# Hybrid RWKV-7 / short-convolution block with top-4-of-32 experts: GpSimd gathers expert rows two rounds ahead, in the middle of the round, and scatters behind that

## What is computed

```python
logits = xf @ w_router + b_router                 # 32 experts
top_v, top_i = lax.top_k(logits, 4); gates = softmax(top_v)
# assignments are grouped by expert, in blocks of up to 128 rows
xb = xf[toks]                                     # rows of one expert
gt = minimum(xb @ w_e_gate[e] + b_e_gate[e], 7)
up = clip(xb @ w_e_up[e] + b_e_up[e], -7, 7)
act = (up + 1) * (gt * sigmoid(1.702 * gt))
y = (act @ w_e_down[e] + b_e_down[e]) * wts[:, None]
out = zeros.at[row_tok].add(y)
```

## Time and profile before

| | before |
|---|---|
| median of 3 runs | 3091.75 us |
| the profiled execution | 3067.25 us |
| its span | 3065.6 us |
| PE busy | 2798.6 us (91%) |
| DVE busy | 1789.7 us (58%) |
| ACT busy | 1361.6 us (44%) |
| POOL busy | 514.2 us (17%) |
| mean granted TensorE clock | 0.955 |

### The profile page before, as it was taken

One profiled execution on the slowest core, in us unless ns is written; L12 is line 12 of the kernel. 1 busy time (PEld: TensorE's weight loads), 2 busy tenths in 40 slices (PEclk: granted clock), 3 DMA queues, 4 the chain that ended last, 5 costly groups with the idle time before them and its releaser, 6 DMA issues.

```text
span 3065.6 us, 55893 instructions
## 1 busy us (share of the span) xinstructions
PE 2798.6 (91%) x21371; PEld 2340.7 (76%) x21371; DVE 1789.7 (58%) x1990; ACT 1361.6 (44%) x1501; POOL 514.2 (17%) x511
## 2 busy tenths in 40 slices
PE   7999999999998999796899999999899999999993
PEld 6797878878898999443688878888777777777772
DVE  3456546464422121143576776767788888888885
ACT  2423232232211111032565666665666666666664
POOL 1010101010000000123132323232222212222220
PEclk9999999999999999897899999999999999999996
DMA  3000000000012110522677868777988888988887
GB/s 105 21 2 15 8 8 15 2 22 1 28 41 56 41 41 21 156 67 70 230 280 257 282 248 283 257 281 264 352 324 323 323 327 330 353 331 329 327 331 245
DMA packets 143212, 536.25 MB, mean 175 GB/s; under 512 B 17633, under 2 KB 71239, under 8 KB 90125
## 3 DMA queue, kind: packets, MB, share of 16 engines
q1 hardware_dynamic: 122925, 492.74, 43.4%
q0 software_dynamic: 20192, 42.08, 5.6%
HBM read 500.35 MB, written 34.42 MB: 174 GB/s over the span
## 4 chain that ended last, share of the span: by engine, by line
PE 71%; DMA 14%; issue 7%; DVE 3%; POOL 2%; ACT 2%; POOLq 1%; SPq 0%; ACTq 0%; DVEq 0%
PE bank L839 30%; PE bank L1958 8%; PE bank L1959 7%; PE bank L1960 7%; DMA x_rows<-hn_d,next_t 6%; DMA next_t<-slot_d 5%; PE bank L1967 5%; PE bank L1871 4%; PE bank L1936 2%; PE bank L835 2%; POOL mid_t L1496 2%; PE bank L915 2%; DMA wo_t<-in_w_o 1%; PE bank L1946 1%; PE bank L2028 1%
## 5 line engine op out<-in xcount | busy, mean ns | idle before, releaser
L1789 DVE TENSOR_TENSOR w_lo<-raw_first,w_hi 128x2048 fp32r<-128x2048 f32 x275 | 618.3, 2283 | 73.7 <-ACT w_hi L1584 73.6
L1584 ACT ACTIVATE w_hi<-raw_first 128x2048 fp32r<-128x2048 f32 x276 | 529.5, 1919 | 228.1 <-DMA raw_first<-in_w_e_up 63.4
L1958 PE MATMUL bank<-w_hi,x_hi 128*128 128x512 f32 x1088 | 434.0, 399 | 2.4 <-ACT yo_rows L1632 2.4
L1959 PE MATMUL bank<-w_lo,x_hi 128*128 128x512 f32 x1088 | 425.1, 391 | 0.0
L1960 PE MATMUL bank<-w_hi,x_lo 128*128 128x512 f32 x1088 | 424.8, 390 | 0.0
L1789 DVE TENSOR_TENSOR w_lo<-raw_rest,w_hi 128x2048 fp32r<-128x2048 f32 x136 | 307.8, 2282 | 0.2
L1584 ACT ACTIVATE w_hi<-raw_rest 128x2048 fp32r<-128x2048 f32 x136 | 260.8, 1917 | 100.8 <-PE bank L1994 43.4
L839 PE MATMUL bank<-xm_hi,ring_hi 128*128 128x260 f32 x896 | 261.9, 292 | 16.2 <-DVE dz L791 8.2
L839 PE MATMUL bank<-xm_lo,ring_hi 128*128 128x260 f32 x896 | 255.0, 285 | 0.0
L839 PE MATMUL bank<-xm_hi,ring_lo 128*128 128x260 f32 x896 | 255.0, 285 | 0.0
L1958 PEld LDWEIGHTS bank<-w_hi,x_hi 128*128 128x128 f32 x1088 | 204.8, 188 | 51.2 <-issue 10.4
(11 more groups left out here) (364 smaller groups left out, 4706.3 us busy)
## 6 DMA issues: line engine op xcount, KB each, us to landing
raw_first<-in_w_e_up SPq DMA_DIRECT2D x138, 1024.0 KB, 5.9
raw_first<-in_w_e_gate SPq DMA_DIRECT2D x70, 1024.0 KB, 6.4
raw_rest<-in_w_e_gate SPq DMA_DIRECT2D x70, 1024.0 KB, 5.6
raw_first<-in_w_e_down SPq DMA_DIRECT2D x68, 1024.0 KB, 6.3
raw_rest<-in_w_e_down SPq DMA_DIRECT2D x68, 1024.0 KB, 8.7
ring<-in_w_in SPq DMA_DIRECT2D x40, 512.0 KB, 3.9
hn_d<-hn SPq DMA_DIRECT2D x10, 416.0 KB
h_d<-h_all SPq DMA_DIRECT2D x10, 416.0 KB
```

The source lines that it names most:

```text
L1584: nc.scalar.activation(w_hi[:, j % NRING, :, :], raw_piece(j), ACT.Copy).then_inc(hi_done, 1)
L1789: nc.vector.tensor_tensor(w_lo[:, j % NRING, :, :], raw_piece(j), w_hi[:, j % NRING, :, :].bitcast(f32), ALU.subtract).then_inc(lo_done, 1)
L1958: nc.tensor.matmul(ps[:, :], hi, w_hi[:, slot, k, :], start=start and k == 0, stop=False)
L1959: nc.tensor.matmul(ps[:, :], hi, w_lo[:, slot, k, :], start=False, stop=False)
```

## The change

GpSimd now asks in the middle of round r for the rows of round r + 2, right after TensorE has transposed those of round r + 1. A second gather stands ahead of the loop. The order in a round becomes: wait for the scatter of round r - 1, copy to `slot_t`; wait for the rows of round r + 1, copy to `mid_t`; wait for the transposes of round r + 1's rows; `gather(r + 2)`; wait for piece 9, biases of round r + 1; scatter round r. No buffer and no transfer is added but one further gather, past the last round.

```diff
         gather(0, True)
         get_biases(0)
+        pool.wait_ge(rows_in[0], 16)
+        pool.wait_ge(rows_in[1], 16)
+        nc.gpsimd.tensor_copy(mid_t, next_t).then_inc(mid_kept, 1)
+        nc.gpsimd.tensor_copy(mid_ov, next_ov).then_inc(mid_kept, 1)
+        pool.wait_ge(mid_kept, 2)
+        pool.wait_ge(xT_ps[3], 1)
+        gather(1, True)
         pool.wait_ge(h_out, 16 * NT)
         for first, last, wide in ((0, n_wide, True), (n_wide, rounds, False)):
             with pool.Fori(first, last) as r:
-
-                pool.wait_ge(rows_in[0], r * 16 + 16)
...
-                pool.wait_ge(xT_ps[3 if wide else 1], r + 1)
-                gather(r + 1, wide)
 
                 pool.wait_ge(y_out[0], r * 16 + 16)
                 pool.wait_ge(y_out[1], r * 32 + 32 if wide else n_wide * 32 + 32)
...
+                pool.wait_ge(rows_in[0], r * 16 + 32)
+                pool.wait_ge(rows_in[1], r * 16 + 32 if wide else n_wide * 16 + 32)
                 pool.sem_inc(pool_passed, 1)
+                nc.gpsimd.tensor_copy(mid_t, next_t).then_inc(mid_kept, 1)
+                if wide:
+                    nc.gpsimd.tensor_copy(mid_ov, next_ov).then_inc(mid_kept, 1)
+                    pool.wait_ge(mid_kept, r * 2 + 4)
+                else:
+                    pool.wait_ge(mid_kept, r + n_wide + 3)
+                pool.sem_inc(pool_passed, 1)
+
+                pool.wait_ge(xT_ps[3 if wide else 1], r + 2)
+                gather(r + 2, wide)
 
                 if wide:
                     pool.wait_ge(ov_used, r * NPIECE + 10)
...
-        pool.wait_ge(rows_in[0], rounds * 16 + 16)
+        pool.wait_ge(rows_in[0], rounds * 16 + 32)
```

## The result

The changed kernel takes 3035.72 us (median of 4 runs, 3033.07 to 3046.09) against 3087.54 for the kernel before (4 runs, 3081.65 to 3095.08). The ratio is 0.9837, 95% interval 0.9802 to 0.9872: faster by 52 us or 1.6%, where 16 us were forecast. The profiled execution took 3033.96 us, 33 less than the profiled one of before. From the scatter on, the code stands five lines further down: L1535 is the L1530 of before, L1941 is L1936 and L1999 is L1994.

What follows compares the result with a forecast made beforehand. PE was taken to bound the wide rounds; in single rounds a scatter-list-gather-PE loop made PE wait, with PE, DMA engines and VectorE near each other. Terms -90 + 74 = -16 us from 3091.75 gave 3076, range 3003 to 3132.

Steps and rivals of the forecast that it cites:

- its loop from scatter to scatter: Single rounds: scatter, list, gather, PE, scatter form a loop that sets the round at 41.1 us.
- The list, behind it in the same queue, lands about 1 us later: Single rounds: the scatter lands at 2500.8, the list about 1 us later, so the gather is issued only at 2502.62.
- Term 1: Single rounds: the wait for gathered rows goes, round 41.1 to 36.8 us, -90 us over 21 rounds (bounds -115 to -44).
- Term 2: Wide rounds: bias load behind the gather comes late, stall 4.0 us plus 1.7 for the clock, +74 us over 13 rounds.
- The rest is moved at no cost: Scatter, copies, SyncE's loads and GpSimd's instruction count: the remaining moves in the round cost 0.
- Biases in time in the wide rounds: Rival, wide rounds: the bias load causes no stall, giving 3002 us; chance 0.20.
- Biases late in the single rounds: Rival, single rounds: biases come 1.5 us late, plus 1.7 for the clock, +67 us, giving 3143; chance 0.17.
- the cover of 2 us: Single rounds: biases land 15.1 us behind the transposes' end, PE wants them at 17; cost 0.
- The DMA engines as the bound: Rival, single rounds: DMA engines hold the round at 39.0 us, -44 + 74 = +30, giving 3122; chance 0.13.

Runs made afterwards that it cites:

- experiment 8: Kernel before, GpSimd's order untouched; in single rounds PE transposes the next rows ahead of piece 10 instead of 8: 2977.78 us against 3083.68, ratio 0.9664.
- experiment 4: Kernel before, with the list for the next round read by ScalarE on its own queue: 3093.27 us, ratio 1.0086.
- experiment 5: Kernel before, with the scatter of the single rounds cut to 16 of its 128 rows: 3052.58 us beside 3080.68.
- experiment 7: Kernel after, loading only half of each weight piece in the single rounds: 3037.55 us.
- Experiment 1: Kernel after, with the biases loaded ahead of the wait for the transposes and the gather, in both loops: 2975.29 us against 3064.4, ratio 0.9695.
- experiment 2: Kernel after, with the bias load issued between the list reads and the two indirect gathers: 2974.31 us, ratio 0.9699.
- experiment 6: Kernel before, loading only half of each weight piece in the single rounds: 2995.36 us beside 3080.68.
- experiment 3: Order of the kernel before in the wide rounds, changed order in the single ones, one gather between the loops: 2961.74 us against 3064.4, ratio 0.9666.
- Experiment 9: Kernel after, with the bias load moved behind the scatter as the last thing of the round: 3335.57 us beside 3080.68.

## Why the prediction was right, and where it was off

**The forecast.** 3076 with a range of 3003 to 3132; measured 3036, inside, and on the side that had the largest chance. The sum was -16 and the medians say -52, so it is right in its two main terms and off in size. Of the 36 us between, 18 are term 1, -5 are term 2, 4 are what counting rounds leaves of the 33 between the profiled executions, and 19 are the spread between executions of before, which the forecast had no term for. By its own two terms as measured it would have come to -29; that the median lies near the low end of the forecast's own range of 3035 to 3115 is in part luck.

**What bounds the kernel.** The forecast's reading, a wait for the rows in every single round and no wait in the wide ones, held, and so did its loop from scatter to scatter: the chain under experiment 8 goes round it. But what is in the loop is the scatter's issue, since GpSimd takes the copy and the list only behind it, and not its landing. "The list, behind it in the same queue, lands about 1 us later" is true of the times and reads as a cause. As a cause it fell: in a queue of its own the list took 8.2 us (experiment 4), and with the scatter landing 4.4 us earlier it came 1.2 us earlier (experiment 5). The list takes 7.0 us because of the weight loads and the scatter in flight together, and 4.6 with half of the one or without the other (the table under experiment 7). The forecast wanted 2 to 4 us for it after the change and it was 4.6. The number wasn't harmed, because the term came from the stall and the clock.

**Term 1** was forecast at -90 and is -108. The term of the sum that was mis-sized is the round that is left, 36.8 us, from a floor of 36.3 us of DMA work and an allowance for two full resources. The round takes 35.94 us, less than that floor, with the same bytes in it (331 x 41.1 against 381 x 35.9). The allowance was for nothing: half the traffic leaves the round at 35.93 (experiment 7). And the share was no measure of work: with 54% of the bytes (205 against 381 GB/s) the share was still 0.65 against 0.99, 66%. The other half of the step, the stall, was read from one round. Its 3.8 us is 3.5 on average (73.6 / 21), and 41.1 - 3.5 - 1.7 = 35.9 us is what was measured, 0.3 above the forecast's 35.6 for TensorE.

**Term 2** was forecast at +74, with +79 in the traces, and is right in mechanism as well; that it is so close is partly luck, as two sizes off by 0.5 and 1.5 us and one round too many offset each other. Issue of the bias load: 6.6 us behind the list (1588.22 - 1581.66), forecast 1892.0 for a list at about 1885, so 7; from the end of the transposes, 7.9 us (1588.22 - 1580.29) against 8.4. Landing: PE goes on 7.3 us behind the issue, near the upper of the two values named (7.7), where 5.8 was taken. Stall 4.65 us (4.0), and 58.4 - 51.8 - 4.65 = 1.9 us of clock and others (1.7). Experiment 1 takes only the bias load out of its place, and 5.2 us a round come back. By the Trainium skill (DMA: Bandwidth & Descriptors, Anatomy of one DMA) the landing would have been 2.1 us, an estimate from its fit, and the term +4. In the wide rounds of these kernels no bias load comes near that (4.9 us at the least, experiment 2); with half of the weight loads, in the single rounds of experiment 6, it was 2.9. The Trainium skill (DMA: Bandwidth & Descriptors, Queues, rings and completion order) leaves room for a later transfer to complete before an earlier one. No run here shows a bias load doing so: it was slower by 2.1 us behind the gathers than ahead of them, by 2.5 behind the full scatter than behind a small one, and landed 0.2 us behind the full one.

**"The rest is moved at no cost"** stands half open. The gather's new place in the wide rounds seemed to cost 1.4 us: 53.2 us in experiment 1 against 51.9 in experiment 3, whose medians lie 13.5 us apart in one set of runs. But 53.0 to 53.7 us, with the same wait for `a_lo`, were also seen where the wide loop was untouched. Which of them it is, the runs don't settle. For the single rounds the statement held: they take 35.94 us with PE busy all the time.

**The rivals.** Biases in time in the wide rounds: refuted, 12 waits. Biases late in the single rounds: no such wait in the first profile of the kernel after, and two short ones of 1.6 and 0.2 us in the second, at the start of the single rounds; how much of the cover of 2 us was left isn't shown, as no view gives the landing there. Experiment 9 is the price when it doesn't hold. The DMA engines as the bound: refuted by half the loads in the kernel after (experiment 7).

**Left open.** The rounds give -29, the profiled executions -33 and the medians -52 and -50. The profiled execution of before is 20 us under the median of that set, and the changed kernel's is 2 under, so most of the difference lies in which execution was profiled. That the slower executions of before have wide rounds of some 53.4 us is the likeliest reading, argued from other kernels with the same loop, and not shown on before itself. Nor is it shown what makes them so. Open as well is by what way the scatter in flight slows a small load, its place in the queue or its traffic.

## What to carry to other kernels

When a step is moved up in an in-order queue, look at what it now stands ahead of: here the rows came in time, and 24 KB of biases behind them came 4.7 us late in every wide round. Give each loop its own order, since the wide loop had no wait to remove. Where the chain of work closes on itself from one round to the next, any piece taken off it helps until the next bound is reached, so compare with the plainer remedy of using the late data later, which gained as much (0.9664) without touching the queue. A transfer that lands just behind another need not be waiting for it; change the other's size, the queue and the traffic beside it before building on it, and ask of each edit what else on the chain it makes shorter.

## What the runs showed of the hardware

- A read of 1 KB took 2.0 us with few other transfers under way. Beside the weight loads it took 4.6 with no scatter in flight, 5.8 with one of 16 rows, 7.0 with one of 128 rows, and 8.2 in ScalarE's own queue with that scatter in flight. With half of the weight loads it took 4.6 with the scatter and 3.2 without. At the same size, what else was moving decided, and a queue of its own didn't help.
- A bias load of 24 KB took, in the wide rounds, 5.2 us behind the list, 5.8 with nothing ahead and 7.3 behind two gathers; in the single rounds 4.6 with nothing ahead (before), 2.9 so with half of the weight loads, 9.0 behind a scatter of 128 rows and 6.5 behind one of 16.
- The DMA engines' share rose from 0.88 to 0.99 with 15% more bytes a second (331 to 381 GB/s), and at 0.65 with 54% of the bytes the round was as long. The share didn't tell how much room was left.
- PE's stall of 4.92 us in a wide round was followed by the lower clock, 0.50 in both windows of 2 us behind its end at 1595.53, and so was the stall of 10.1 us in experiment 9, with 0.50 and 0.54.
